# Prompt differential attention with 64-row score tiles, a hand-over by 512-key pieces, and the output scaling on ACT

## The reference

```python
def diff_weighted_values(q, k, v, qpos, kpos, valid, lam):
    s = jnp.einsum('bihmd,bjhmd->bhmij', q, k,
                   preferred_element_type=jnp.float32) * (HEAD_DIM ** -0.5)
    dist = jnp.abs(qpos[:, None] - kpos[None, :]).astype(jnp.float32)
    s = s - alibi_slopes(B_HEADS)[:, None, None, None] * dist
    if valid is not None:
        s = jnp.where(valid, s, NEG_INF)
    p = jax.nn.softmax(s, axis=-1)
    a = p[:, :, 0] - lam * p[:, :, 1]
    return jnp.einsum('bhij,bjhe->bihe', a.astype(v.dtype), v)
```

## Time and profile before

| | before |
|---|---|
| median of 3 runs | 954.0 us (949.71 to 955.08) |
| the profiled execution | 951.99 us, span 950.2 us |
| busy over the span | PE 90%, DVE 42%, ACT 32%, POOL 24% |
| mean granted TensorE clock | 0.961 |
| `diff_prompt` | 365.48 to 483.16 us of the span |

### The profile page before, as it was taken

How to read it: one execution, slowest core, us unless ns; L and a number is a source line. 1 busy time by engine, 2 the same in 40 slices (tenths; PEclk the granted TensorE clock), 3 DMA queues, 4 the chain that set the end, 5 groups by cost and what they waited for, 6 DMA issues and landing times. The chain is left out here.

```text
span 950.2 us, 14047 instructions
## 1 busy us (share of the span) xinstructions
PE 854.6 (90%) x5391; PEld 773.3 (81%) x5391; DVE 403.1 (42%) x884; ACT 299.7 (32%) x606; POOL 228.0 (24%) x217
## 2 busy tenths in 40 slices
PE   4799999999999998999989986656599999889998
PEld 3799999999999996776679964444499997478998
DVE  6831111111011115888777752322342434985744
ACT  6221110111110004566668853121431111553111
POOL 6353332221122211212211210220222210652220
PEclk9999999999999999999999997777799999899999
DMA  7022221222221201000063025898271100010311
GB/s 299 23 98 91 94 95 70 95 91 75 94 70 45 75 0 46 1 1 0 0 236 135 1 63 226 318 357 320 70 297 63 43 25 1 22 67 23 123 69 75
DMA packets 28851, 92.51 MB, mean 97 GB/s; under 512 B 4088, under 2 KB 9208, under 8 KB 27640
## 3 DMA queue, kind: packets, MB, share of 16 engines
q1 hardware_dynamic: 26208, 81.18, 23.3%
q10 hardware_dynamic: 2592, 10.62, 2.7%
HBM read 76.12 MB, written 16.58 MB: 98 GB/s over the span
## 5 line engine op out<-in xcount | busy, mean ns | idle before, releaser
L207 PE MATMUL in_acc<-in_x_hi,w_hi 128*128 128x384 f32 x312 | 107.4, 344 | 19.4 <-DVE in_x_lo L440 18.9
L208 PE MATMUL in_acc<-in_x_lo,w_hi 128*128 128x384 f32 x312 | 106.6, 342 | 0.0
L209 PE MATMUL in_acc<-in_x_hi,w_lo 128*128 128x384 f32 x312 | 106.5, 341 | 0.0
L207 PE MATMUL in_acc<-in_x_hi,in_w_hi 128*128 128x384 f32 x312 | 105.0, 337 | 0.0
L209 PE MATMUL in_acc<-in_x_hi,in_w_lo 128*128 128x384 f32 x312 | 104.3, 334 | 0.0
L208 PE MATMUL in_acc<-in_x_lo,in_w_hi 128*128 128x384 f32 x312 | 104.2, 334 | 0.0
L207 PEld LDWEIGHTS in_acc<-in_x_hi,w_hi 128*128 128x128 f32 x312 | 59.3, 190 | 21.6 <-issue 18.7
L207 PE MATMUL mrg_acc<-mrg_a_hi,w_hi 128*128 128x384 f32 x192 | 67.1, 349 | 6.1 <-issue 3.0
L802 ACT ACTIVATE arena<-arena,diff_nmax 128x128 f32<-128x128 f32 (+7 forms) x64 | 49.4, 772 | 66.6 <-DVE diff_nmax L758 66.4
L710 PE MATMUL diff_score<-kT,diff_q_slot 128*128 (+4 forms) x192 | 67.6, 488 | 2.7 <-PEq L231 2.1
L209 PE MATMUL mrg_acc<-mrg_a_hi,w_lo 128*128 128x384 f32 x192 | 65.4, 341 | 0.0
(11 more groups left out here) (230 smaller groups left out, 1642.3 us busy)
## 6 DMA issues: line engine op xcount, KB each, us to landing
qo<-xT SPq DMA_DIRECT2D x16, 576.0 KB, 9.1
kT<-kb_cache SPq DMA_DIRECT2D x4, 2048.0 KB, 8.9
v_tok<-vb_cache SPq DMA_DIRECT2D x4, 2048.0 KB, 7.8
arena<-kb_cache SPq DMA_DIRECT2D x4, 2048.0 KB, 11.3
arena<-vb_cache SPq DMA_DIRECT2D x4, 2048.0 KB, 7.3
w_raw<-w_in SPq DMA_DIRECT2D x13, 512.0 KB, 3.4
in_w_raw<-w_in SPq DMA_DIRECT2D x13, 512.0 KB, 3.5
z_scratch<-in_squares ACTq DMA_DIRECT2D x8, 576.0 KB, 2.8
```

Of the source, the lines that this page charges most:

```text
L207: pe.matmul(out, w_hi, x_hi, start=start, stop=False)
L208: pe.matmul(out, w_hi, x_lo, start=False, stop=False)
L209: return pe.matmul(out, w_lo, x_hi, start=False, stop=stop)
```

## The change

The change does five things inside `diff_prompt`.

1. `scores` takes the 64 rows of each map from `qo` and `kT` in place: a matmul of map 0 uses partitions 0 to 63, one of map 1 partitions 64 to 127. The zero-padded slots, POOL's `zero` and `place`, and the semaphore between POOL and PE go.
2. Scores are handed over by pieces of up to 512 keys, both maps of a piece under one count of `scored`. For tiles with more than 512 keys DVE reduces each piece of each map by itself (4 reductions in place of 2), and a new step `top` takes the smaller of the two partial minima. The scores of a piece wait only for the readers of that piece.
3. `exponent` waits for both maps (for `top` from tile 4 on), and for `coef` of the item two before in place of its `weigh`.
4. DVE's order becomes bias(i), invert(i-1), top(i), factor(i-1), weigh(i-1); `take` moves to ACT, behind `clear`, as a scaled copy with lag 3.
5. All 32 items are written out (`unrolled`) in place of the loop over heads. POOL's memsets and first copies for `window_prompt` come at the start of the block.

```diff
+def unrolled(last, period, steps):
+    for newest in range(last * period + max(lag for lag, _ in steps)):
+        for lag, step in steps:
+            at = newest - lag
+            if 0 <= at < last * period:
+                step(at // period, at % period)
...
@@ project, block.gpsimd
             pool.wait_ge(w_lo_done, NB_IN)
-            diff_q.zero(pool)
-            pool.wait_ge(diff_q.zeroed, 4)
-            pool.wait_ge(evacuated, 2 * G_Q + NQ // 2 + 1)
-            for t in range(2):
-                diff_q.place(pool, 0, t)
...
@@ diff_prompt
+        part = [[mk.sb(f"part{i}{p}", [P, 2]) for p in range(2)] for i in range(2)]
...
+        def pieces(t):
+            return [(c, min(512, (t + 1) * P - c)) for c in range(0, (t + 1) * P, 512)]
+        def biased_through(h, t, c):
+            return 2 * (PER_HEAD * h + banks_before[t] + c + 1)
+        def last_reader(h, t, c):
+            item = 8 * h + t - 1
+            while item >= 0 and len(pieces(item % NT)) <= c:
+                item -= 1
+            return biased_through(item // NT, item % NT, c) if item >= 0 else 0
+        def topped_through(h, t):
+            return 4 * h + max(0, t - 3)
...
@@ block.gpsimd
-            def place(h, t):
-                if isinstance(h, int) and h == 0 and t < 2:
-                    return
-                pool.wait_ge(scored, 2 * (8 * h + t) - 2)
-                diff_q.place(pool, h, t)
-
-            stages(pool, BH, NT, [(0, place)])
-            pool.wait_ge(q_ready, 2 * BH * NT)
             window_q.zero(pool)
             ahead.zero_own(pool)
...
             def scores(h, t):
-                for m in range(2):
-                    pe.wait_ge(q_ready, 2 * (8 * h + t) + m + 1)
-                    wait(pe, biased, 2 * (8 * h + t) + m - 1)
-                    for c in range(0, (t + 1) * P, 512):
-                        n = min(512, (t + 1) * P - c)
-                        last = pe.matmul(score[m][:, c:c + n], slot[t % 2][m][:], kT[:, h + 1, c:c + n],
-                                         start=True, stop=True)
+                for i, (c, n) in enumerate(pieces(t)):
+                    wait(pe, biased, last_reader(h, t, i))
+                    for m in range(2):
+                        rows = slice(m * HD, (m + 1) * HD)
+                        last = pe.matmul(score[m][:, c:c + n], qo[rows, BH + h, t * P:(t + 1) * P],
+                                         kT[rows, h + 1, c:c + n], start=True, stop=True)
                     last.then_inc(scored, 1)
...
-            stages(pe, BH, NT, [(0, scores), (2, turn), (3, average)])
+            unrolled(BH, NT, [(0, scores), (2, turn), (3, average)])
...
@@ bias
-                wait(dve, block_ready, PER_HEAD * h + (banks_before[t - 3] if t >= 3 else
-                                                       banks_before[t + NT - 3] - PER_HEAD))
-                dve.wait_ge(scored, 2 * item + 1)
-                dve.memset(waited[:, 2 * (t % 2):2 * (t % 2) + 1], 0.0)
-                for m in range(2):
-                    if m:
-                        dve.wait_ge(scored, 2 * item + 2)
-                        dve.memset(waited[:, 2 * (t % 2) + 1:2 * (t % 2) + 2], 0.0)
-                    dve.tensor_tensor_reduce(prob[t % 4][:, m, 0:n], score[m][:, 0:n], strip[:, SEQ - n:SEQ],
-                                             1.0, HIGHEST, ALU.add, ALU.min,
-                                             nmax[t % 2][:, m:m + 1]).then_inc(biased, 1)
+                if item >= 4:
+                    back = item - 4
+                    dve.wait_ge(block_ready, PER_HEAD * (back // NT) + banks_before[back % NT + 1])
+                for i, (c, size) in enumerate(pieces(t)):
+                    dve.wait_ge(scored, PER_HEAD * h + banks_before[t] + i + 1)
+                    dve.memset(waited[:, 2 * (t % 2) + i:2 * (t % 2) + i + 1], 0.0)
+                    for m in range(2):
+                        least = (nmax if t < 4 else part[i])[t % 2]
+                        dve.tensor_tensor_reduce(prob[t % 4][:, m, c:c + size], score[m][:, c:c + size],
+                                                 strip[:, SEQ - n + c:SEQ - n + c + size],
+                                                 1.0, HIGHEST, ALU.add, ALU.min,
+                                                 least[:, m:m + 1]).then_inc(biased, 1)
+            def top(h, t):
+                if t >= 4:
+                    dve.wait_ge(biased, biased_through(h, t, 1))
+                    dve.tensor_tensor(nmax[t % 2][:], part[0][t % 2][:], part[1][t % 2][:],
+                                      ALU.min).then_inc(topped, 1)
...
-            def take(h, t):
-                dve.wait_ge(av_done, 8 * h + t + 1)
-                dve.tensor_scalar(o[:, 8 * h + t, :], mixed[t % 2][:, 0:P], inv[t % 4][:, 0:1], None,
-                                  ALU.mult).then_inc(o_done, 1)
-            stages(dve, BH, NT, [(4, take), (0, bias), (1, weigh)])
+            unrolled(BH, NT, [(0, bias), (1, invert), (0, top), (1, factor), (1, weigh)])
...
             def exponent(h, t):
                 item = 8 * h + t
-                wait(act, weighted, item - 1)
+                wait(act, coef_done, item - 1)
                 n = (t + 1) * P
+                if t < 4:
+                    act.wait_ge(biased, biased_through(h, t, 0))
+                else:
+                    act.wait_ge(topped, topped_through(h, t))
                 for m in range(2):
-                    act.wait_ge(biased, 2 * item + m + 1)
...
-            stages(act, BH, NT, [(0, exponent), (2, clear)])
+            def take(h, t):
+                act.wait_ge(av_done, 8 * h + t + 1)
+                act.activation(o[:, 8 * h + t, :], mixed[t % 2][:, 0:P], ACT.Copy,
+                               scale=inv[t % 4][:, 0:1]).then_inc(o_done, 1)
+            unrolled(BH, NT, [(0, exponent), (2, clear), (3, take)])
+            act.wait_ge(o_done, BH * NT)
```

More of the change, by code:

```diff
@@ L569, with __init__ @@
 class DiffQ:
-    def __init__(self, nc, ctx, qo, lam_in, tables):
+    def __init__(self, nc, ctx, lam_in, tables):
         mk = Maker(nc, ctx, "diff_q")
@@ L577, in __init__ @@
         self.neg_lam, self.load_lambda, self.lambda_vector, self.lambda_scalar = neg_lambda(mk, lam_in)
-        self.slot = [[mk.sb(f"slot{p}{m}", [P, P]) for m in range(2)] for p in range(2)]
-        self.zeroed, self.ready, self.qo = mk.sem("zeroed"), mk.sem("ready"), qo
     def load(self, sp):
@@ L583, in load @@
         sp.dma_start(self.strip[:], self.tables["strip"]).then_inc(self.strip_in, 16)
-    def zero(self, pool):
-        for p in range(2):
-            for m in range(2):
-                pool.memset(self.slot[p][m][:], 0.0).then_inc(self.zeroed, 1)
-    def place(self, pool, h, t):
-        for m in range(2):
-            rows = slice(m * HD, (m + 1) * HD)
-            pool.tensor_copy(self.slot[t % 2][m][rows, :],
-                             self.qo[rows, BH + h, t * P:(t + 1) * P]).then_inc(self.ready, 1)
 class WindowQ:
@@ L742, in bias @@
                 item = 8 * h + t
-                if t == 0 and not (isinstance(h, int) and h == 0):
-                    dve.wait_ge(biased, 2 * item)
+                if t == 0 and h > 0:
+                    dve.wait_ge(biased, biased_through(h - 1, NT - 1, 1))
                     dve.tensor_scalar(strip[:], strip[:], 0.25, None, ALU.mult).then_inc(stripped, 1)
@@ L748, in bias, with invert @@
                 n = (t + 1) * P
-                wait(dve, block_ready, PER_HEAD * h + (banks_before[t - 3] if t >= 3 else
-                                                       banks_before[t + NT - 3] - PER_HEAD))
-                dve.wait_ge(scored, 2 * item + 1)
-                dve.memset(waited[:, 2 * (t % 2):2 * (t % 2) + 1], 0.0)
-                for m in range(2):
-                    if m:
-                        dve.wait_ge(scored, 2 * item + 2)
-                        dve.memset(waited[:, 2 * (t % 2) + 1:2 * (t % 2) + 2], 0.0)
-                    dve.tensor_tensor_reduce(prob[t % 4][:, m, 0:n], score[m][:, 0:n], strip[:, SEQ - n:SEQ],
-                                             1.0, HIGHEST, ALU.add, ALU.min,
-                                             nmax[t % 2][:, m:m + 1]).then_inc(biased, 1)
-            def weigh(h, t):
+                if item >= 4:
[15 more added lines that the diff above has]
+                                      ALU.min).then_inc(topped, 1)
+            def invert(h, t):
                 item = 8 * h + t
@@ L766, in weigh, with factor @@
                 dve.reciprocal(inv[t % 4][:], norm[t % 2][:]).then_inc(inv_done, 1)
+            def factor(h, t):
+                item = 8 * h + t
                 dve.wait_ge(inv_done, item + 1)
@@ L769, in weigh @@
                                          in1=norm[t % 2][:, 0:1], op0=ALU.mult, op1=ALU.mult).then_inc(coef_done, 1)
+            def weigh(h, t):
+                item = 8 * h + t
                 dve.wait_ge(coef_done, item + 1)
```

6 lines of the change are left out of this document (2 added, 4 removed).

## The result

The changed kernel takes 956.63 us (median of 20 runs, 951.2 to 961.71), the kernel before 953.27 in the same sessions (20 runs, 948.01 to 955.08). The ratio is 1.0039, 95% interval 1.0023 to 1.0056: 0.4% slower, where 0.3% faster was forecast. The time lies inside the range of 944 to 959, on the other side of no change.

The account below looks back on a forecast made before the run. PE was taken as the bound, busy 27.91 of 28.78 us a head. Head gains of 2.05, 1.0 and 1.0 less a last-head loss of 0.8 gave 3.2 us, so 951.0 against 954.0; range 944 to 959.

Parts of the forecast that it names:

- PE's costs: PE at tile 7: four slots 1.72, six transposes 0.65, ten average records 1.11, two switches 0.40, together 3.88 us.
- A pair is one slot: PE's scores: two 64-row tiles run side by side in one 0.43 us slot, scores falling from 15.5 to 7.7 us a head.
- The rival of 1.3 slots: PE's scores: the two tiles of a pair hinder each other, 3.4 us more in all, total 954; chance 0.10.
- changes of form: PE switching between 128*128 and 64*128 tiles in every item: 0.20 us each way, 0.40 an item; bounds 0 and 0.30.
- DVE's stretch: Tile 4 to the next head's tile 0: DVE sets it at 14.95 us against 17.00, a gain of 2.05.
- Tile 0 to tile 4: First half of a head: PE stays the bound and pays the switches, 12.85 us against 11.78, a loss of 1.07.
- 0.87 us wait: PE's wait for ACT's copy between tiles 0 and 1, kept at today's 0.87 us within that step's 3.79 us.
- the hand-over from tile 3 to 4: Serial step on one copy of the scores: reductions 1.25, two slots 0.86, tail, semaphore and load 0.35, together 2.46 us.
- the rival in which the engines come close to their own sums: Waits hide behind the largest engine of each item: head near 25.9 us, 12 us less in all, half way 946; chance 0.23.
- The clock: PE's granted clock in the block stays 1.00; rival: it falls to 0.80, up to 10 us more, 961; chance 0.04.
- a block below 1.00: Stated sign of being wrong: the block's granted clock in the changed profile lies below 1.00.
- The written-out loop at nothing: Fetching the longer code of 32 written-out items costs nothing: the already written-out first head takes 16.99 us against 17.00 later.

Follow-up runs that it names:

- copies first: The changed kernel with ACT's copies of item i-2 put ahead of its exponentials, nothing else changed: 942.6 us, ratio 0.9894 to the kernel before.
- whole maps handed over: The kernel before with 64-row tiles, scores handed over a map at a time and output scaling moved to ACT: 944.52 us, ratio 0.9889.
- copies first and filler: The changed kernel with ACT's copies ahead of its exponentials and an unused matmul pair after each of the first three scores: 941.09 us, ratio 0.9893.
- the padded rows back: The changed kernel with scores taken from the zero-padded 128-row slots again, copied by POOL, all else kept: 973.09 us in one run.
- the tiles with whole maps: The kernel before with 64-row tiles and whole-map hand-over: plain 947.57 us, with scaling on ACT 944.52, with ACT's copies ahead of its exponentials 942.59.
- the tiles alone: The kernel before with only the 64-row tiles and PE's loop written out, scores still handed over a whole map at a time: 947.57 us, ratio 0.9952.

## Why the prediction was wrong, step by step

**PE's costs: right.** A pair is one slot. The rival of 1.3 slots, by proportion from the four row tiles of the Trainium skill (TensorE: Matmul & The Clock Gate, "Measured speedup vs the span model"), is refuted for pairs of 64 rows in this number format: 0.43 us for two. Scores, transposes, averages and two changes of form at tile 7 were put at 3.88 us; in the run with copies first, where PE doesn't wait, they take 3.92 (436.54 to 440.46), where the sum without the changes of form is 3.48.

**DVE's stretch: right, with some luck.** Tile 4 to the next tile 0 was put at 14.95 us; in the third head it is 14.74. But 0.49 of that is waiting that goes with copies first (14.25), so DVE's own work was put some 0.7 too high, and a wait that the sum did not have made up for most of it.

**Tile 0 to tile 4: the wait was mis-sized.** 12.85 us were forecast, 13.47 measured. The step that failed is that the 0.87 us wait is "kept since ACT's order is the same". The order is the same, but what stands first in it comes later: `exponent` begins after the last piece of the second map and `top`, and the copies behind it are late with it. The prediction named the copies as queued behind `exponent` and then gave them no price. The wait is 1.76 us at tile 0, and there is a second one at tile 7 (1.02), mostly hidden beside DVE's stretch. Of the 0.62 us, 0.46 lie between tiles 0 and 1 (4.25 for 3.79) and 0.22 in the hand-over from tile 3 to 4 (2.68 for 2.46). So at full clock the third head gains 0.57 us and not 1.0; the second, where the wait at tile 0 is 2.17, gains 0.15. That this is the cause is shown from both sides: with the copies moved ahead, or with whole maps handed over, the stop at tile 7 is gone and the head is 26.06 or 26.42. The one at tile 0 stays in part: 1.36 us for the copies with whole maps, and with copies first PE waits there for DVE's `weigh` instead, 1.57 us, and DVE then waits only 0.24 for PE. So without the late copies PE does not set the time from tile 0 to tile 1, as the forecast had it; DVE does. The 26.06 us of that head are near the 25.9 of the rival in which the engines come close to their own sums, and the argument against that rival, two exponentials ahead of the copy, is the obstacle that the swap removes.

**The clock: the assumption that turned the sign.** The granted clock of 1.00 was carried over from before, and its fall was a rival with a chance of 0.04, priced from the sample block at up to 10 us; a block below 1.00 was one of the prediction's own signs of being wrong, and it came (0.94). In four profiles of the change the clock is at 1.2 GHz for 10 to 14 us of the first head and at one or two boundaries. Head by head, the forecast was -2.05, -1.0, -1.0 and +0.8 us; the first profile has +2.36, -0.15, -0.57 and +2.23, in sum +3.87 for -3.2. Of the first head's 4.4 us of error the low clock accounts for about 2.9: from tile 1 to tile 5, the stretch of the fall, it takes 12.48 us (366.51 to 378.99) against 9.54 in the run with copies first and filler, at full clock (366.01 to 375.55). The rest is not the clock. Even in that run, whose filler may add to it, tile 0 to tile 4 of the first head takes 8.08 us against 7.24 before, where the prediction set the changes of form against POOL's waits, and so at nothing. The last head's 1.4 is the fall at 449.40, the like of those that cost 1.6. Without the two falls the block would be about 4.5 us shorter, an estimate from these differences, and so 0.6 below the one before: the falls turned the sign, and the waits and the unpriced part of the first head ate most of the 3.2. The prediction judged PE by its share of a whole head, 82%, and that was about right (23.56 of 28.21, 84%). But the idle time is not spread over the head: it lies where ACT's copies are late and where the first head's small tiles wait for their reductions, and there PE is busy about half of the time.

The two errors meet at the boundary: late exponentials make late copies, these make PE stand, and as the stop ends the clock may fall. That it is the stop, and not the lighter load, the other runs show: with the padded rows back PE is as loaded as before, and the clock falls behind all three boundaries; in the three profiles of the tiles with whole maps PE is relieved, and no boundary has a fall (with the tiles alone it stands 1.36 to 1.40 us there). Copies first shortens the block by 8.7 us between the profiles (121.55 to 112.81) and the median by 14.7. Its profile has no fall at a boundary where the longer executions of the change have two; against the block of the longest of these (125.92) it gains 13.1 us. How the median's 14.7 divides is not accounted for further, since a median has no profile.

**The written-out loop at nothing** was not tried by itself, so its price is not shown; the tiles alone have PE's loop written out, and gained.

**Left open.** Why the clock falls at one boundary and not at another: 417.70 to 421.20 in the first profile has PE busy for the same 1.74 of 3.50 us as the third boundary, and no fall behind it; and with copies first PE still stands 1.57 us at a boundary without one. Why DVE's own work was put 0.7 too high stays open as well. And why the sample block takes 116 us in one execution and 121 in another.

## What to carry to other kernels

When a change moves TensorE's waits, work out its busy share stretch by stretch and not over the whole loop: behind a stretch in which it newly stands idle, its clock may fall, and the loss can exceed the gain. When a wait moves later on an in-order engine, price everything queued behind it, and ask whether what others wait for can stand ahead of it. A finer hand-over helps only if its consumer starts earlier by it: here the exponentials needed the minimum over all pieces, so they started later.

## What the runs showed of the hardware that was not expected

At the head boundaries TensorE's granted clock fell to 1.2 GHz though PE had not stood for longer than 2.2 us (2.17 ahead of 394.0), and the same kernel took from 949 to 962 us, by tendency the longer the lower its mean clock (0.952 at 951.2 us, 0.935 at 961.71). The Trainium skill (TensorE: Matmul & The Clock Gate, "A second HAM failure mode: psum-queue depth-cycling") describes a clock that swings because the engine idles briefly between groups of matmuls; the trace agrees that no long idle time is needed, though here it is one or two waits of 1 to 2.2 us at a boundary. Some 2.8 us of useless matmuls a head, all in idle time, with three more pairs at the block's start, made the kernel 8 us faster.
